# Differential heads' norm on the Scalar engine, rotations summed from PSUM, and a new order of the first block's tables, spreads and scores

## Chip, cores and metric

One core of a Trainium2 chip runs the whole program. The metric is the device time in microseconds of one execution, the median of several.

## What is computed

A three-layer stack on x of 512 tokens by 1024 channels, in fp32. Cut to what the change bears on:

```python
# first block
h = rms_norm(x, norm_mix); proj = h @ w_in            # pool, lru, q, k, v, gates
qh = rms_norm(q.reshape(B, S, 8, 128), q_norm)        # kh alike
z = qh @ kh.T * scale                                 # per head, causal
log_beta, log_keep = log_sigmoid(z), where(causal, log_sigmoid(-z), 0)
w = where(causal, exp(log_beta + reverse_cumsum_after(log_keep)), 0); y = w @ v
# ... pooling and LRU branches, gates, w_out, gated ffn
# even layer: MoBA attention (8 heads of 64) and differential attention (4 heads)
p = softmax(s)                                        # two score maps per head
o = rmsnorm((p[:, :, 0] - lam * p[:, :, 1]) @ v, subln_g) * (1 - lam_init)
# odd layer: dilated attention (8 heads of 64) and MLA (4 heads)
q = rmsnorm(cq, q_norm) @ w_uq                        # nope 128, rope 64 per head
rope(x) = [x1 * cos - x2 * sin, x1 * sin + x2 * cos]  # on q's rope part and on kr
# a convolutional ffn after each of both layers, then a last rmsnorm
```

## The kernel before

Channels lie on the 128 partitions (P) and the 512 tokens (S) in the free dimension; x is 8 tiles of 128x512 (KT = 8), and tokens are also counted in 4 blocks of 128 (NB). Each engine has its own program, written out by hand, and the programs meet at semaphores that count events. So the order of work on each engine is the order of the code, and an instruction that waits holds all behind it.

A product of full accuracy is three fp32r products of a high and a low part (L408 to L410, in the helper `products`). The high parts of the weights are made by ACT (L1306, in `refill`; L1428 while attention runs), the low parts by POOL (L1138), one slice of 128x2048 at a time, from raw weights that SP's DMA queue brings into two buffers.

**First block.** PE's loop over chunks of the value projection (i = 0, 1, with 4 blocks b of tokens, c for halves) weaves in the sums of squares of q and k (`qk_sum`, L852), and for i = 1 the 16 `qk_spread` products (L897), 2 per step: the reciprocal roots of 16 rows lie as high and low parts in rows 0 to 15 and 32 to 47 of `qkrstd`, the other rows being zero, and a product with a column of `both` spreads one of them over 128 partitions. DVE's `qk_norm` (L2221) then scales a tile of q or k, which gives `qk_normed`. ACT scales the values out of the banks (L1626, `v_read`), calling `refill` after each four. Then `sb_scores` (L938) of heads 0 and 1, products for the gates, `softplus` on ACT (L1642 to L1648), `sb_sums` (L950, L954), `sb_weights` (L1654). `token_scales` (L443) makes, in three places of the program, a column per block of tokens out of the row `rstd`; DVE copies it (L1862).

**Even layer.** Units g = 0 to 7 are the two score maps of each of the four differential heads, 8 to 15 are MoBA (`MOBA` = 8). For every head and block b of queries PE runs `transposes` of the merged weights, the scores of the next head's two units, `head_fill` (products of MoBA's queries, L408 to L410), and the products with the values (L655). ACT makes exponents (L1396) and copies even blocks of transposed weights from PSUM (L1418); DVE makes maxima (L1947), copies odd blocks (L1965, `copy_odd`), merges the two maps (L1974, L1975 and an addition) and, with `head_normalised`, scales the output by the sums. The norm of a head is `head_squares` (L1990, L1991, DVE), `diff_scales` (Ln and Exp, ACT) and `diff_normed` (L2007, DVE); `head_turn` then turns the head's tokens back (L726) on PE, ahead of both units of b = 2 one head later.

**Odd layer.** Units 16 to 23 are dilated attention (`DIL` = 16), 24 to 27 MLA. `SLOTS` is a table of what PE weaves in between the 32 steps (g, b) of the dilated units: `uq` products of MLA's queries in two halves (4 and 5 are the rope parts), `rot` the rotation product (0 for the keys, 1 and 2 for the queries, L762), `oturn` a turn of finished output, `uk` and `uv` keys and values. Results go to banks 7 and 2 in turn, in the order of `SPARE`, which all engines look up. ACT copies a finished `uq` out (`mla_copy`, L1516); DVE finishes a rotation in `rotated` (L2100, L2103, L2104: rotated part times sines, plain part times cosines, sum), at the step of its slot and ahead of the next `copy_odd`. `stack_low`, `key_low` and swaps of halves run on POOL (L1192, L1201).

## Time and profile before

| | us |
|---|---|
| median of 3 runs | 2227.19 (2226.87 to 2228.06) |
| the profiled execution | 2227.95 |
| its span | 2226.1 |
| busy PE, DVE, ACT, POOL | 2190.9, 875.4, 828.7, 1037.4 |

Rows of a timeline are: start, duration, engine, line, operation, out<-in, shapes, count, and in brackets the idle time of the engine before it with what ended it. MATMUL rows have modelled ends. PEld is the weight loads of PE. The span's average granted clock is 0.997 of full.

### The profile page before, as it was taken

What the parts mean: (1) busy time and instruction counts of PE and PEld (TensorE: products, weight loads), DVE (VectorE), ACT (ScalarE), POOL (GpSimd) and SP (SyncE); (2) the same over time, 40 slices, a digit from 0 to 9 for tenths busy, and PEclk for the clock granted to TensorE, in tenths of its full rate; (3) what the DMA queues carried; (4) which work ended last, traced back from release to release, by engine and by line L of the source; (5) the groups of instructions that cost most, each with busy time, mean ns of one, the idle gap of its engine ahead of it and who ended that gap; (6) DMA issues with size and microseconds to landing.
All of it is one profiled execution on the core that took longest, in us unless ns stands there. A gap on an engine that the chain in (4) does not pass through costs nothing. (4 is left out here: it accounts for less than half of the span.)

```text
span 2226.1 us, 27528 instructions
## 1 busy us (share of the span) xinstructions
PE 2190.9 (98%) x10090; PEld 1796.6 (81%) x10090; DVE 875.4 (39%) x1346; ACT 828.7 (37%) x1135; POOL 1037.4 (47%) x872
## 2 busy tenths in 40 slices
PE   8999999999999999999999999999999999999998
PEld 6768877888888888888878888888887788888887
DVE  6334576633351111222377533232225646332212
ACT  4235565422242222222246433332224634333321
POOL 5441144555554444555444354445554524444543
PEclk9999999999999999999999999999999999999999
DMA  5221122332223222333212222222332212222232
GB/s 172 92 77 57 42 91 77 113 107 99 97 76 113 94 94 77 104 103 108 96 54 66 76 95 94 101 89 91 100 120 90 72 48 95 94 95 94 84 104 77
DMA packets 33991, 201.88 MB, mean 91 GB/s; under 512 B 3900, under 2 KB 6204, under 8 KB 15484
## 3 DMA queue, kind: packets, MB, share of 16 engines
q1 hardware_dynamic: 31532, 192.94, 25.5%
q0 software_dynamic: 2384, 7.92, 1.2%
q8 instruction: 50, 0.82, 0.2%
q14 instruction: 25, 0.20, 0.0%
HBM read 198.69 MB, written 2.15 MB: 90 GB/s over the span
## 5 line engine op out<-in xcount | busy, mean ns | idle before, releaser
L1138 POOL TENSOR_TENSOR w_low<-raw,w_high 128x512 fp32r<-128x512 f32 (+2 forms) x768 | 959.8, 1281 | 1056.5 <-ACT w_high L1306 1013.4
L408 PE MATMUL bank<-x_low,w_high 128*128 128x512 f32 x1728 | 684.8, 396 | 10.7 <-DVE x_low L2141 9.3
L409 PE MATMUL bank<-x_high,w_high 128*128 128x512 f32 x1728 | 673.9, 390 | 0.0
L410 PE MATMUL bank<-x_high,w_low 128*128 128x512 f32 x1728 | 673.9, 390 | 0.0
L1306 ACT ACTIVATE w_high<-raw 128x2048 fp32r<-128x2048 f32 (+1 forms) x183 | 327.3, 1788 | 544.2 <-PE bank L410 544.2
L408 PEld LDWEIGHTS bank<-x_low,w_high 128*128 128x128 f32 x1728 | 325.3, 188 | 83.2 <-POOL w_low L1232 9.2
L409 PEld LDWEIGHTS bank<-x_high,w_high 128*128 128x128 f32 x1728 | 325.3, 188 | 70.4 <-issue 3.1
L410 PEld LDWEIGHTS bank<-x_high,w_low 128*128 128x128 f32 x1728 | 325.2, 188 | 68.6
L408 PE MATMUL bank<-act_low,w_high 128*128 128x512 f32 (+1 forms) x550 | 209.4, 381 | 0.0
L409 PE MATMUL bank<-act_high,w_high 128*128 128x512 f32 (+1 forms) x550 | 209.3, 381 | 0.0
L410 PE MATMUL bank<-act_high,w_low 128*128 128x512 f32 (+1 forms) x550 | 209.3, 380 | 0.0
L1928 DVE TENSOR_TENSOR temp_b<-temp_a,bank 128x512 f32<-128x512 f32 x66 | 45.4, 687 | 230.3 <-PE bank L410 229.9
L1371 ACT ACTIVATE act_high<-temp_b 128x512 f32 x66 | 41.8, 633 | 216.2 <-DVE temp_b L1928 216.0
L409 PEld LDWEIGHTS bank<-act_high,w_high 128*128 128x128 f32 x550 | 103.4, 188 | 19.8
L408 PEld LDWEIGHTS bank<-act_low,w_high 128*128 128x128 f32 x550 | 103.4, 188 | 19.8
L410 PEld LDWEIGHTS bank<-act_high,w_low 128*128 128x128 f32 x550 | 103.4, 188 | 19.7
L1882 DVE TENSOR_TENSOR gate_scaled<-bank,rstd 128x512 f32<-128x512 f32 x23 | 15.9, 692 | 257.2 <-PE bank L410 257.2
L1360 ACT ACTIVATE temp_a<-gate_scaled,columns 128x512 f32<-128x512 f32 x44 | 35.7, 816 | 157.9 <-DVE gate_scaled L1912 157.9
L1396 ACT ACTIVATE probs<-probs,small 128x128 f32<-128x128 f32 (+1 forms) x96 | 53.9, 561 | 100.6 <-DVE small L1947 100.2
L1912 DVE TENSOR_TENSOR gate_scaled<-bank,rstd 128x512 f32<-128x512 f32 x44 | 30.2, 691 | 152.7 <-PE bank L410 152.3
L408 PE MATMUL bank<-y_low,w_high 128*128 128x512 f32 x208 | 82.5, 397 | 0.0
L409 PE MATMUL bank<-y_high,w_high 128*128 128x512 f32 x208 | 80.9, 389 | 0.0
(284 smaller groups left out, 2745.9 us busy)
## 6 DMA issues: line engine op xcount, KB each, us to landing
raw<-wmain SPq DMA_DIRECT2D x144, 1024.0 KB, 4.9
raw<-wdown SPq DMA_DIRECT2D x48, 704.0 KB, 4.0
bias<-distance_table POOLq DMA_DIRECT2D x24, 256.0 KB, 3.4
raw<-wmain SPq DMA_DIRECT2D x4, 512.0 KB, 8.7
x_residual<-x SPq DMA_DIRECT2D x4, 512.0 KB, 7.4
out<-qk SPq DMA_DIRECT2D x8, 256.0 KB, 2.2
matrices<-mats SPq DMA_DIRECT2D x1, 512.0 KB, 11.5
r_blocks<-rg POOLq DMA_DIRECT2D x1, 512.0 KB, 6.4
```

The costliest lines, as they stand in the source:

```text
L408: pe.matmul(target, sh, ml, start=start and k == 0, stop=False)
L409: pe.matmul(target, sh, mh, start=False, stop=False)
L410: last = pe.matmul(target, sl, mh, start=False, stop=stop and k == n - 1)
L1138: pool.tensor_tensor(wl[:, c, part], raw[:, c, part], wh[:, c, part].bitcast(F32), ALU.subtract).then_inc(low_ready, 1)
L1306: act.activation(wh[:, c, 0:width], raw[:, c, 0:width], ACT.Copy).then_inc(high_ready, 1)
L1360: act.activation(tmpa[:, j, :], gs[:, j, :], ACT.Identity, bias=col("ffn_b", i * 2 + (k + j)), scale=col("ffn_w", i * 2 + (3 * k + 2 * FT ...
L1371: act.activation(tile(ah, i * 2 + j), tmpb[:, j, :], ACT.Copy).then_inc(sem("f_high"), 1)
L1396: act.activation(probs(g, b), probs(g, b), ACT.Exp, bias=nm[:, u, b:b + 1], scale=-1.0, accum_out=rs[:, u, b:b + 1]).then_inc(sem("p_ready ...
L1882: dve.tensor_tensor(gs[:, t % 2, :], bank[banks[t]][:, :], rstd[:, :], ALU.mult)\
L1912: dve.tensor_tensor(gs[:, j, :] if n else tmpa[:, j, :], bank[j][:, :], rstd[:, :], ALU.mult)\
L1928: dve.tensor_tensor(tmpb[:, j, :], tmpa[:, j, :], bank[2 + j][:, :], ALU.mult)\
```

## The change

- `token_scales`: four transposes of a 128x128 block of `rstd` instead of four fp32 products with one column; DVE's copy takes every 128th column.
- The spreads' operands have all 128 rows instead of 48; three spreads per step from the first step of i = 1 on instead of two per step.
- `sb_scores(0)` waits for 7 evictions of values instead of 8. ACT's table for Ln and Exp is loaded behind the Sqrt of `qk_std`; the second `refill` is moved behind `softplus(0)`.
- A differential head's norm: per block of tokens a Square with an accumulated sum, then Ln and Exp (b = 0 of the next head), then per block a Copy with a scale (b = 1), all on ACT; both DVE steps are gone. PE's `head_turn` is between the two units of b = 2. The ratio in `merge` is a tensor_scalar.
- Rotations: `key_parts` and `query_parts` on DVE multiply by cosines and by sines first, the queries straight from PSUM; PE rotates the sine part; `rotated` is one addition from PSUM. The order in `SLOTS` and `SPARE` follows.

```diff
@@ -81,7 +81,7 @@
              + [("eturn", 2), ("eturn", 3)] + [("eout", t) for t in range(6)]
-             + [("uq", 4), ("uq", 5), ("rot", 0), ("uq", 0), ("oturn", 0), ("rot", 1), ("uq", 1), ("rot", 2), ("uq", 2)]
+             + [("rot", 0), ("uq", 4), ("uq", 5), ("rot", 1), ("oturn", 0), ("uq", 0), ("rot", 2), ("uq", 1), ("uq", 2)]
              + [("oturn", 1), ("uq", 3)] + [("uk", j) for j in range(4)] + [("uv", 0), ("uv", 1), ("oturn", 2)]
@@ -89,10 +89,10 @@
 NONE = (None, 0, ())
-SLOTS = [("uq", 4, (0, 1)), ("uq", 5, (0,)), ("uq", 5, (1,)), NONE]
-SLOTS += [("rot", 0, ()), ("uq", 0, (0,)), ("uq", 0, (1,)), NONE]
-SLOTS += [("oturn", 0, ()), ("rot", 1, ()), ("uq", 1, (0,)), ("uq", 1, (1,))]
-SLOTS += [("rot", 2, ()), ("uq", 2, (0,)), ("uq", 2, (1,)), NONE]
+SLOTS = [("rot", 0, ()), ("uq", 4, (0,)), ("uq", 4, (1,)), NONE]
+SLOTS += [("uq", 5, (0,)), ("uq", 5, (1,)), ("rot", 1, ()), NONE]
+SLOTS += [("oturn", 0, ()), ("uq", 0, (0,)), ("uq", 0, (1,)), ("rot", 2, ())]
+SLOTS += [("uq", j, (k,)) for j in (1, 2) for k in range(2)]
 SLOTS += [("oturn", 1, ()), ("uq", 3, (0,)), ("uq", 3, (1,)), ("uk", 0, ())]
@@ -171,8 +171,8 @@
     ident_r, negtri_r, negones_r, negmask_r = (exact[:, j, :] for j in range(4))
-    qkrstd = over("qk_rstd_parts", [48, S], 40, F32R)
-    both = over("both_parts", [48, 16], 42.25, F32R)
+    qkrstd = over("qk_rstd_parts", [P, S], 40, F32R)
+    both = over("both_parts", [P, 16], 42.25, F32R)
@@ -194,7 +194,7 @@
-    turned = place("turned_rope", [P, S], at=mla_qk_at + KT * S * 4)
+    sines = place("sine_parts", [P, 2, S], at=mla_qk_at + KT * S * 4)
     qs_r = over("q_stage_r", [P, 2, S], 38, F32R)
@@ -440,8 +440,8 @@
                 for b in range(NB):
-                    last = pe.matmul(bank[target][:, b:b + 1], rstd[:, b * P:(b + 1) * P], ident[:, 0:1],
-                                     start=True, stop=True)
+                    tokens = slice(b * P, (b + 1) * P)
+                    last = pe.transpose(bank[target][:, tokens], rstd[:, tokens], ident)
                 last.then_inc(sem("token_scales"), 1)
@@ -618,7 +618,7 @@
                         spare_free(pe, ("uv", 2), ("uv", 3))
-                        pe.wait_ge(sem("roped"), 3)
+                        pe.wait_ge(sem("roped"), 9)
                     pe.matmul(target, mla_qk[:, 2 * m + u, q], mla_qk[:, 4 + 2 * m + u, 0:n], start=True, stop=False)
@@ -664,7 +664,7 @@
                 target = spare(("eturn", h))
-                pe.wait_ge(sem("y_token"), h + 1)
+                pe.wait_ge(sem("y_token"), 4 * h + 4)
                 turn(target, 4 + h).then_inc(sem("spare_ready"), 1)
@@ -680,9 +680,9 @@
                         transposes(2 * h, b)
-                        if 0 < h < HEADS - 1 and b == 2:
-                            head_turn(h - 1)
                         for u in range(2):
+                            if 0 < h < HEADS - 1 and b == 2 and u == 1:
+                                head_turn(h - 1)
                             if h < HEADS - 1:
@@ -757,9 +757,8 @@
-                if n:
-                    spare_free(pe, ("uq", 3 + n))
-                pe.matmul(spare(("rot", n)), small_rot, qk[:, 11 + n, :], start=True, stop=True)\
+                pe.wait_ge(sem("roped"), (2, 5, 7)[n])
+                pe.matmul(spare(("rot", n)), small_rot, sines[:, n - 1, :] if n else pts[:, 1, :], start=True, stop=True)\
                   .then_inc(sem("spare_ready"), 1)
@@ -894,7 +893,7 @@
                     pe.wait_ge(sem("qk_rstd"), 1)
-                pe.matmul(bank[4 + n % 4][:, :], both[:, t:t + 1].to_broadcast([48, P]), qkrstd[:, :], start=True,
+                pe.matmul(bank[4 + n % 4][:, :], both[:, t:t + 1].to_broadcast([P, P]), qkrstd[:, :], start=True,
                           stop=True).then_inc(sem("qk_spread"), 1)
@@ -917,8 +916,9 @@
                         if i == 1:
-                            qk_spread(8 * c + 2 * b)
-                            qk_spread(8 * c + 2 * b + 1)
+                            at = 4 * c + b
+                            for n in range(min(3 * at, 16), min(3 * at + 3, 16)):
+                                qk_spread(n)
@@ -931,7 +931,7 @@
                 else:
-                    pe.wait_ge(sem("v_read"), 8)
+                    pe.wait_ge(sem("v_read"), 7 + h)
                     pe.wait_ge(sem("qk_normed"), 16)
@@ -1163,7 +1163,7 @@
                         spare_free(pool, ("uq", 2), ("uq", 3))
-                        pool.wait_ge(sem("roped"), 3)
+                        pool.wait_ge(sem("roped"), 9)
                     pool.tensor_copy(gs[half, u, :], qk[half, n + 12, :]).then_inc(sem("rope_staged"), 1)
@@ -1456,8 +1456,10 @@
                             exponent(MOBA, b)
-                        if h and b == h // 3:
+                        if h and b == 0:
                             diff_scales(h - 1)
+                        if h and b == 1:
+                            diff_normed(h - 1)
                         if 0 < h < HEADS - 1 and b == 2:
@@ -1476,18 +1478,31 @@
                         spare_out(g, b)
-                        if (g, b) == (MOBA, 1):
+                        if (g, b) == (MOBA, 0):
                             diff_scales(3)
+                        if (g, b) == (MOBA, 2):
+                            diff_normed(3)
                         if b % 2:
...
                 d = dss[:, 4 * h:4 * h + 4]
-                act.wait_ge(sem("diff_squares"), h + 1)
+                act.wait_ge(sem("y_read"), h + 1)
+                for q in range(NB):
+                    act.activation(tmpa[:, 1, q * P:(q + 1) * P], yt[:, q, (4 + h) * P:(5 + h) * P], ACT.Square,
+                                   accum_out=d[:, q:q + 1]).then_inc(sem("diff_squares"), 1)
+                act.wait_ge(sem("diff_squares"), 4 * h + 4)
                 act.activation(d, d, ACT.Ln, bias=col("eps", 0), scale=1.0 / P).then_inc(sem("diff_scale"), 1)
...
                 act.activation(d, d, ACT.Exp, scale=-0.5).then_inc(sem("diff_scale"), 1)
+
+            def diff_normed(h):
+
+                act.wait_ge(sem("diff_scale"), 2 * h + 2)
+                for q in range(NB):
+                    y = yt[:, q, (4 + h) * P:(5 + h) * P]
+                    act.activation(y, y, ACT.Copy, scale=dss[:, 4 * h + q:4 * h + q + 1]).then_inc(sem("y_token"), 1)
@@ -1529,8 +1544,8 @@
                     kind, n, ks = SLOTS[at]
-                    if kind == "uq" and 1 in ks:
-                        mla_copy(("uq", n), qk[:, 8 + n, :] if n >= 4 else mla_qk[:, n, :], scale=192 ** -0.5)
+                    if kind == "uq" and n < 4 and 1 in ks:
+                        mla_copy(("uq", n), mla_qk[:, n, :], scale=192 ** -0.5)
                     elif kind == "oturn":
@@ -1620,12 +1635,14 @@
                     act.activation(gs[0:16, 0, :], gs[0:16, 0, :], ACT.Sqrt).then_inc(sem("qk_std"), 1)
+                    act.preload_act_table_set("natural_log_exp_and_others")
                 for b in range(NB):
...
                        .then_inc(sem("v_read"), 1)
-                refill(1, n0 + 2 * i + 1)
+                if i == 0:
+                    refill(1, n0 + 1)
             act.wait_ge(table_stored, 16)
@@ -1658,8 +1675,9 @@
-            act.preload_act_table_set("natural_log_exp_and_others")
             softplus(0)
+            act.wait_ge(sem("v_ready"), 10)
+            refill(1, n0 + 3)
             softplus(1)
@@ -1859,7 +1877,7 @@
                 dve.wait_ge(sem("token_scales"), n)
-                dve.tensor_copy(token_rstd, bank[source][:, 0:NB]).then_inc(sem("token_copied"), 1)
+                dve.tensor_copy(token_rstd, bank[source][:, 0:S:P]).then_inc(sem("token_copied"), 1)
                 dve.wait_ge(sem("token_copied"), n)
@@ -1972,7 +1990,7 @@
                 step(dve.reciprocal(rd2, rs[:, :, b:b + 1]))
-                step(dve.scalar_tensor_tensor(ratio, rs[:, 0, b:b + 1], nlam, rd2[:, 1, :], ALU.mult, ALU.mult))
+                step(dve.tensor_scalar(ratio, rs[:, 0, b:b + 1], nlam, rd2[:, 1, :], ALU.mult, ALU.mult))
                 dve.scalar_tensor_tensor(probs(2 * h, b), probs(2 * h + 1, b), ratio, probs(2 * h, b), ALU.mult,
@@ -1982,13 +2000,6 @@
                                   ALU.mult).then_inc(sem("y_read"), 1)
-
-            def head_squares(h):
-
-                y, w = yt[:, :, (4 + h) * P:(5 + h) * P], blocks(tmpa[:, 1, :])
-                dve.wait_ge(sem("y_read"), h + 1)
-                step(dve.tensor_tensor(w, y, y, ALU.mult))
-                dve.tensor_reduce(dss[:, 4 * h:4 * h + 4].unsqueeze(2), w, AX.X, ALU.add).then_inc(sem("diff_squares"), 1)
@@ -1999,13 +2010,6 @@
                    .then_inc(sem("y_read"), 1)
-
-            def diff_normed(h):
-
-                dve.wait_ge(sem("diff_scale"), 2 * h + 2)
-                y = yt[:, :, (4 + h) * P:(5 + h) * P]
-                dve.tensor_tensor(y, y, dss[:, 4 * h:4 * h + 4].unsqueeze(2).to_broadcast([P, NB, P]), ALU.mult)\
-                   .then_inc(sem("y_token"), 1)
@@ -2039,17 +2043,11 @@
                             moba_copy(0)
-                        if h == HEADS - 1 and b == 0:
-                            head_squares(h - 1)
-                        if h and b == 1 + h // 3:
-                            diff_normed(h - 1)
                         if 0 < h < HEADS - 1 and b == 3:
...
                     head_normalised(h)
-                    if h < 2:
-                        head_squares(h)
@@ -2064,10 +2062,6 @@
                             stack_low(g + 2, b - 1)
-                        if (g, b) == (MOBA, 0):
-                            head_squares(3)
-                        if (g, b) == (MOBA, 2):
-                            diff_normed(3)
                         spare_out(g, b)
@@ -2091,18 +2085,31 @@
+            def key_parts():
+
+                x = qk[:, 11, :]
+                dve.wait_ge(sem("rope_landed"), 16)
+                dve.tensor_tensor(pts[:, 1, :], x, rope[:, 1, :], ALU.mult).then_inc(sem("roped"), 1)
+                dve.tensor_tensor(x, x, rope[:, 0, :], ALU.mult).then_inc(sem("roped"), 1)
+
+            def query_parts(n):
+
+                use = ("uq", 3 + n)
+                dve.wait_ge(sem("spare_ready"), SPARE[use] + 1)
+                dve.scalar_tensor_tensor(qk[:, 11 + n, :], spare_bank(use), 192 ** -0.5, rope[:, 0, :], ALU.mult, ALU.mult)\
+                   .then_inc(sem("roped"), 1)
+                dve.scalar_tensor_tensor(sines[:, n - 1, :], spare_bank(use), 192 ** -0.5, rope[:, 1, :], ALU.mult,
+                                         ALU.mult).then_inc(sem("roped"), 1)
+                dve.wait_ge(sem("roped"), 2 * n + 3)
+                dve.sem_inc(spare_read(use), 1)
+
             def rotated(n):
-                x, use = qk[:, 11 + n, :], SPARE["rot", n]
-                if n == 0:
-                    dve.wait_ge(sem("rope_landed"), 16)
-                dve.wait_ge(sem("spare_ready"), use + 1)
-                dve.tensor_tensor(turned[:, :], spare_bank(("rot", n)), rope[:, 1, :], ALU.mult)\
-                   .then_inc(spare_read(("rot", n)), 1)
-                spare_free(dve, ("rot", n))
-                step(dve.tensor_tensor(x, x, rope[:, 0, :], ALU.mult))
-                dve.tensor_tensor(x, x, turned[:, :], ALU.add).then_inc(sem("roped"), 1)
-                dve.wait_ge(sem("roped"), n + 1)
+                x, use = qk[:, 11 + n, :], ("rot", n)
+                dve.wait_ge(sem("spare_ready"), SPARE[use] + 1)
+                dve.tensor_tensor(x, x, spare_bank(use), ALU.add).then_inc(spare_read(use), 1)
+                spare_free(dve, use)
+                dve.sem_inc(sem("roped"), 1)
@@ -2115,11 +2122,13 @@
                     at = 4 * (g - DIL) + b
-                    kind, n, _ = SLOTS[at]
+                    kind, n, ks = SLOTS[at]
                     if at and SLOTS[at - 1][0] == "oturn":
...
                         rotated(n)
+                    elif kind == "uq" and n >= 4 and 1 in ks:
+                        query_parts(n - 3)
                 elif (g, b) == (MLA, 1):
@@ -2204,7 +2213,7 @@
             dve.sem_inc(table_ready, 1)
-            step(dve.tensor_tensor(both[:, :], ident[0:48, 0:16], ident[0:48, 32:48], ALU.add))
+            step(dve.tensor_tensor(both[:, :], ident[:, 0:16], ident[:, 32:48], ALU.add))
             step(dve.memset(qkrstd[:, :].bitcast(F32), 0.0))
@@ -2391,6 +2400,7 @@
                 stack_low(g, 1)
+            key_parts()
             dve.wait_ge(sem("c_sum"), 3)
...
                 dve.tensor_scalar(tq[:, 2 + t, :], bank[6 + t][:, :], 1.0 / (2 * P, P)[t], EPS, ALU.mult, ALU.add)\
```

## Rows read from the trace of the kernel before

**Rows 1.** Part 1 of the page: busy time, share of the span, instructions.
```profile
PE 2190.9 (98%) x10090; PEld 1796.6 (81%) x10090; DVE 875.4 (39%) x1346; ACT 828.7 (37%) x1135; POOL 1037.4 (47%) x872
```
**Rows 2.** Timeline of PE and its weight loads, a pair of spreads (start, us, ...).
```profile
155.80 0.39 PE L409 MATMUL bank<-w_high,x_high 128*128 128x512 f32 x1
156.02 0.39 PE L410 MATMUL bank<-w_high,x_low 128*128 128x512 f32 x1
156.34 0.29 PEld L897 LDWEIGHTS bank<-qk_rstd_parts,both_parts 48*128 48x128 f32 x2 [0.35 <-issue]
...
157.34 0.40 PE L409 MATMUL bank<-w_high,x_high 128*128 128x512 f32 x1
```
**Rows 3.** Timeline of PE: scores of heads 0 and 1, and a later head's.
```profile
159.63 0.39 PE L410 MATMUL bank<-w_high,x_low 128*128 128x512 f32 x1
...
162.03 6.24 PE L938 MATMUL bank<-qk 128*128 128x512 f32 x16 [1.35 <-DVE qk L2221]
167.93 0.58 PE L408 MATMUL bank<-x_low,w_high 128*128 128x512 f32 x1
...
208.37 2.32 PE L938 MATMUL bank<-qk 128*128 128x512 f32 x8
210.52 2.32 PE L964 MATMUL bank<-sb_weights,v_tokens 128*128 128x512 f32 x8
```
**Rows 4.** Timeline of ACT between the values and the first softplus.
```profile
160.64 1.90 ACT L1306 ACTIVATE w_high<-raw 128x2048 fp32r<-128x2048 f32 x1
162.56 1.28 ACT L1661 ACT_TABLE_LOAD   x1
```
**Rows 5.** Windows: busy us of PE, PEld, DVE, ACT, POOL; PEclk, DMA share, GB/s.
```profile
162.20:165.70 3.50, 3.50 (x7) 1.86 (x7) 0.00 (x0) 2.30 (x4) 3.08 (x3) 0.51 0.00 0
1169.10:1172.60 3.50, 3.48 (x12) 3.18 (x13) 2.56 (x7) 1.97 (x7) 0.00 (x0) 0.51 0.62 255
1140.00:1160.00 20.00, 17.86 (x89) 14.06 (x88) 16.02 (x35) 9.51 (x25) 11.32 (x10) 1.00 0.19 66
```
**Rows 6.** Timeline of PE: the first token_scales.
```profile
75.96 0.95 PE L443 MATMUL bank<-matrices,rstd 128*128 128x1 f32 x8
76.78 0.40 PE L852 MATMUL bank<-square_high,pick_r 128*16 128x512 f32 x1
```
**Rows 7.** Timeline of PE, differential heads: the rows in front of which it waits.
```profile
1129.10 0.63 PE L726 MATMUL bank<-matrices,y_tokens 128*128 128x128 f32 x4 [0.57 <-DVE y_tokens L2007]
...
1150.59 0.63 PE L726 MATMUL bank<-matrices,y_tokens 128*128 128x128 f32 x4 [2.14 <-DVE y_tokens L2007]
...
1169.12 1.20 PE L655 MATMUL bank<-v_tokens,probs_t 128*128 128x128 f32 x4 [3.13 <-DVE probs_t L1965]
...
1187.81 1.77 PE L655 MATMUL bank<-v_tokens,probs_t 128*128 128x64 f32 x14 [0.83 <-ACT probs_t L1418]
```
**Rows 8.** Timeline of DVE in the differential heads.
```profile
1160.25 0.22 DVE L1975 SCALAR_TENSOR_TENSOR small<-small 128x1 f32<-128x1 f32 x1
...
1163.36 1.21 DVE L1975 SCALAR_TENSOR_TENSOR small<-small 128x1 f32<-128x1 f32 x1
...
1166.27 1.74 DVE L1990 TENSOR_TENSOR temp_a<-y_tokens 128x512 f32<-128x512 f32 x1
```
**Rows 9.** Timeline of ACT in the differential heads: an exponent of 128x128.
```profile
1143.32 0.40 ACT L1396 ACTIVATE probs<-probs,small 128x128 f32<-128x128 f32 x1 [2.17 <-DVE small L1947]
```
**Rows 10.** PE's waits in 1712 to 1751: us in total, times, longest.
```profile
PE bank L655 <- DVE probs_t L1965: 1.8, 2, 1.2
PE bank L655 <- ACT probs_t L1418: 1.7, 3, 0.6
PE bank L408 <- DVE qk_r L2085: 0.7, 1, 0.7
```
**Rows 11.** Timeline of DVE, dilated stage: rotated's third operation.
```profile
1726.81 1.66 DVE L2104 TENSOR_TENSOR qk<-qk,turned_rope 128x512 f32<-128x512 f32 x1
```
**Rows 12.** ACT by lines, 1238 to 1268: count, busy us and mean ns, idle before.
```profile
L1323 ACT ACTIVATE temp_a<-x_residual 128x512 f32<-128x512 f32 x8 | 4.9, 616 | 0.0
```

## Prediction, written before the changed kernel was run

> **What bounds the kernel now.** I read the page's busy shares first: PE is busy for 98% of the span, each other engine for less than half of it [rows 1]. So only what PE does or waits for can move the end, and I went on to PE's waits, then to the timeline of the three places that the diff touches. One caution for all of it: a 512-column product starts 0.22 to 0.23 us after the one before (155.80, 156.02), though its row shows 0.39, with a modelled end [rows 2]. An idle in a row is counted from that late end, so a stall costs about 0.17 more than the row says. I sum starts, not idles.
>
> **Part 1, first block.** *Spreads.* Two `qk_spread` products run between products in each block of tokens. From 156.02 to 157.34 is 1.32 us, in which the pair and two products start; four at 0.227 would be 0.91. The other 0.41 goes with the 0.35 that stands, as "issue", in front of the weights' load of 48 rows [rows 2]; loads of 128 rows around it have none. With 128 rows the load has its neighbours' form, so I drop 0.41 for the 7 pairs ahead of the last: **2.9 us** (bounds 0, and 3.3 for all 8). The Trainium skill, "TensorE: Matmul & The Clock Gate", section "Step-by-step: what each phase is for", speaks against it: load time goes by columns, and the number of rows doesn't matter. By that rule this term is 0 and the time 2.9 higher; the 0.35 in front of the 48-row load is what I go by.
>
> *The gap.* With three spreads per block, the last pair leaves the place where it delays everything. From 159.63 to 162.03 is 2.40 us where 0.23 is the pace; 0.45 of it is the pair, which runs earlier now: 2.40 - 0.23 - 0.45 = **1.7 us** [rows 3]. The wait inside it, 1.35 for DVE's `qk` L2221, goes because the last row is normalised a block earlier, and `sb_scores(0)` no longer stands for the eviction of the last v bank (7 for 8). What is late next is `softplus(0)`: ahead of it on ACT stood a refill of 1.90 and a table load of 1.28 [rows 4]. The load moves to the values' stage, where ACT idles between evictions, and the refill behind `softplus(0)`, so the chain ends about when PE comes to `sb_sums(0)`: 0, and at most 1.9 back if that cover fails. The slice refilled is wanted two heads later: no wait.
>
> *Scores.* The 16 records of heads 0 and 1 take 162.03 to 167.93, 5.90 us; the 8 of a later head 208.37 to 210.52, 2.15, so 16 should take 4.30 [rows 3]. Why: the granted clock is 0.51 of full, 1.2 of 2.4 GHz, for 3.5 us right behind the wait [rows 5]. Without the wait I expect no fall: 1.6 and 0.2 in the product behind, **1.8 us** (bounds 0 and 1.8).
>
> *Tables.* `token_scales` at 75.96 takes 0.82 up to the next start, for 8 one-column records [rows 6]. Four 128-column transposes lie at 0.63 with their modelled tail of some 0.2 (the `head_turn` rows in [rows 7]), so about 0.45: **0.4 us**. At the two later places the copy stands behind DVE's evictions anyway: 0. Part 1: 2.9 + 1.7 + 1.8 + 0.4 = **6.8**.
>
> **Part 2, differential heads.** PE stands here for DVE at 1129.10 (0.57) and 1150.59 (2.14), both for `diff_normed` L2007, and at 1169.12 (3.13), for `probs_t` L1965, which is late because DVE's queue is [rows 7]. With the hidden 0.17 that is 0.74, 2.3 and 3.3. DVE is full: 16.0 of 20 us [rows 5]. The squares L1990 take 1.74, and the ratio L1975 takes 0.22 once and 1.21 three us on, with POOL making low halves beside it [rows 8]. Squares, their sum and `diff_normed` leave DVE, some 3 to 4 us a head. I keep 0.4 of the 2.3 and 0.3 of the 3.3, since the turn now waits for four copies on ACT: 0.74 + 1.9 + 3.0 = 5.6. With the wait at 1169 its half clock goes too, 3.5 us at 0.51 [rows 5]: **1.7**.
>
> ACT gets four squares with their sums and four copies of 128x128 per head. An exponent of that size with the reading of its sum is 0.40 [rows 9]; a copy has no sum to read, an estimate of 0.27: 4 x 0.40 + 4 x 0.27 = 2.7 us a head. ACT was busy for 9.5 of 20 us [rows 5], so this is covered on the average. Where PE already stands for ACT, 0.83 at 1187.81 [rows 7], a little grows: -0.3. On PE `head_turn` moves between the two units of b = 2; behind its new wait (`y_token` 4h + 4) stand the scores of u = 1 and `head_fill`. Part 2: 5.6 + 1.7 - 0.3 = **7.0**, bounds 3 and 9.
>
> *The ratio* as one tensor and two per-partition scalars: between 0 and the 1.0 of [rows 8] a time, already within the 3.0. The Trainium skill, "SBUF — State Buffer", section "Who interferes with whom", says that two SBUF inputs contend with POOL's reads, as 1.21 against 0.22 bears out; but also that tensor_scalar can take the shared port as a whole and then block. By the latter the edit gives nothing, and the time would be some 0.5 higher.
>
> **Part 3, dilated stage (1712 to 1751).** PE's waits are 5.7 us by the rows in ten waits, of which three lines stand in [rows 10]; ten times 0.16 more makes 7.3. (a) The 0.7 for `qk_r` L2085 is that of slot 0, the `uq4` product; now the keys' rotation is first, ready long before: 0.8. (b) The `mla_copy` of `uq4` and `uq5` leave ACT, where they stand ahead of `probs_t` L1418: of three waits (1.7) I drop 1.1. (c) `rotated` is three operations on DVE, of which the last, with both inputs in SBUF, takes 1.66 [rows 11], and a `copy_odd` (L1965) is behind them; one sum from PSUM remains. Both its waits go: 1.8 + 0.3 = 2.1. (d) The wait for L1947: 0.3. Together **4.3**, bounds 2 and 6. What comes instead: `query_parts`, two PSUM operations of some 0.7 each in front of a `copy_odd`; and `key_parts`, ahead of the wait for `c_sum`, which pushes the low halves and the values' evictions by 1.4 us or more, an estimate at the two rates of an SBUF pair. PE wants these later than that. `roped` 9 instead of 3 in the MLA scores is met some units before: 0.
>
> **Sum.** 6.8 + 7.0 + 4.3 = 18.1 off the profiled execution's own 2227.95 gives 2209.85. That execution is 0.76 above the runs' median of 2227.19, so **2209.1**.
>
> **Rivals.** (1) *ACT becomes the bound in the heads.* Squares stand at b = 0 and copies at b = 1, ahead of that block's next exponents and copies, so PE stands for ACT where it stood for DVE; an average of half says nothing of one block. Part 2 is then 0 instead of 7: 2216.1 (2213 to 2219). For it: the 0.83 at 1187.81; against it: 9.5 of 20 us. (2) *DVE or POOL bounds the dilated stage.* The 1.4 us of `query_parts` takes the place of what goes, or POOL's bias and key halves are what is late next, and Part 3 gives 1: 2212.4. (3) *The number of rows is irrelevant*, and the 0.41 comes from the broadcast weights or from the place, which stay: 2209.1 + 2.9 = 2212.0. The skill's rule above would say so. (4) *The clock falls elsewhere*, behind new waits, as often as now: 2209.1 + 3.4 = 2212.5. (5) **Slower:** *the tables of ACT are loaded anew in every head.* If Square or Copy lay in another set than Exp and Ln, each head had two loads at 1.28 [rows 4] with the 2.7 of work between exponents that PE waits for, 5.3 us; times 4 is 21, and Part 2's gain is gone as well: 2209.1 + 7 + 21 = 2237. It decides where ACT's idle in a head is under 5.3 in one piece. Against it: eight Squares of L1323 run between others of ACT with 0.0 idle before them [rows 12], and a load is a row of its own, which that stretch lacks. (6) *The change doesn't do what it says*: new waits hold the moved steps where the old ones did, and Parts 2 and 3 are nil: 2227.2 - 6.8 = 2220.4.
>
> **How the numbers follow.** Main case 0.55 (2205 to 2213.5); (1) 0.17, (2) 0.11, (3) 0.05, (4) 0.04, (5) 0.03, (6) or several together 0.05. A difference under 0.2%, 4.5 us, is about what can't be told from none here. So faster is all under 2222.7: main and (1) to (4), 0.92. Same 0.05: (6) alone would still be a little under that line, but Part 1's lower bounds (0 for the spreads, 0 for the scores) carry it over, and I count it whole. Slower 0.03, from (5). The range takes (1) to (4) in: up to 2218, and down to 2203, where the upper bounds of the three parts (7.2 + 9 + 6 = 22.2, so 2205.0) stand, with 2 us for waits that I haven't counted.
>
> **What would show it.** Right: no "issue" ahead of the spreads' loads; less than 0.5 between the last product and L938 of head 0; a clock of 1.0 in both stretches; no wait of PE for y_tokens over 0.5; the one addition left of `rotated` near 0.7; PE's waits in the dilated stage at 2 or less. Wrong: PE standing for L1418 or L1396 over 2 us in all between 1100 and 1190 (rival 1); table loads in the heads (rival 5); a wait for softplus in front of `sb_sums(0)` of over 0.5; a wait at L628 or L655 of the dilated stage that falls on `query_parts`. What makes all of it wrong is a stretch that the change lengthens where I saw no wait.

## The result and the profile after

The changed kernel takes 2216.84 us (2213.99 to 2217.16, 5 runs) where the kernel before took 2227.19; the ratio is 0.9950, 95% interval 0.9939 to 0.9962. So 10.3 us came off, where 18.1 were forecast. The profiled execution is 2217.16 us with a span of 2215.3, the slowest of the five; beside the profiled 2227.95 of before it is 10.8 less. The page's first part, as [rows 1] before:

```profile
PE 2185.9 (99%) x10078; PEld 1797.6 (81%) x10078; DVE 861.8 (39%) x1334; ACT 838.7 (38%) x1181; POOL 1038.8 (47%) x872
```

DVE lost 13.6 us of work and ACT gained 10.0. What PE stands for is told by its waits over the whole span (us in total, times, longest); the first three lines and those of the places touched:

```profile
PE bank L408 <- DVE x_low L2150: 9.5, 1, 9.5
PE bank L950 <- DVE softplus_low L2270: 2.9, 1, 2.9
PE bank L408 <- PEq L431: 1.9, 2, 1.1
PE bank L655 <- ACT probs_t L1418: 1.6, 3, 0.8
...
PE bank L655 <- DVE probs_t L1983: 1.5, 2, 1.3
...
PE bank L726 <- DVE y_tokens L2010: 0.8, 2, 0.5
```

The waits for `diff_normed` are gone. The second line is new: `sb_sums(0)` stands 2.9 us for DVE.

To see where the time went I took the start of the same product of PE in each trace: the 1401st of its L409 rows, shortly ahead of the differential heads, and the 1501st, shortly behind them. The three stretches that they cut tell the three parts of the change apart:

| us | up to the 1401st | from there to the 1501st | from there to PE's last row |
|---|---|---|---|
| before | 1065.06 | 109.95 | 1044.59 |
| after | 1063.97 | 102.80 | 1041.87 |
| difference | -1.1 | -7.2 | -2.7 |
| forecast | -6.8 | -7.0 | -4.3 |

The heads are right to 0.2 us, the first block is nearly all missing, and the dilated stage lacks 1.6.

One thing has to come off the first column. The first work of PE that the change touches is the first `token_scales`, and PE comes to it at 75.96 before and at 75.29 after, so 0.7 of the 1.1 is a difference of the two executions and not of the change. From there to the 1401st product it is 989.10 us before and 988.69 after: 0.4 less.

**First block, after.** The timeline of PE shows the changed `token_scales`, and three spreads between two products; PE's gap ahead of the scores of head 0 is gone. It answers to [rows 6], [rows 2] and [rows 3]:

```profile
75.29 0.60 PE L444 MATMUL bank<-matrices,rstd 128*128 128x128 f32 x4
75.64 0.48 PE L851 MATMUL bank<-square_high,pick_r 128*16 128x512 f32 x1
...
133.56 0.86 PE L896 MATMUL bank<-qk_rstd_parts,both_parts 128*128 128x512 f32 x3
134.25 0.39 PE L408 MATMUL bank<-w_low,x_high 128*128 128x512 f32 x1
...
156.14 0.39 PE L410 MATMUL bank<-w_high,x_low 128*128 128x512 f32 x1
156.37 4.48 PE L938 MATMUL bank<-qk 128*128 128x512 f32 x16
160.50 0.58 PE L408 MATMUL bank<-x_low,w_high 128*128 128x512 f32 x1
...
169.19 0.50 PE L950 MATMUL bank<-softplus_high,matrices_r 128*128 128x512 f32 x1 [2.85 <-DVE softplus_low L2270]
```

Start to start, `token_scales` takes 0.35 (before 0.82), three spreads 0.69, which is three times the pace, the step from the last product to the scores 0.23, the scores 4.13 (before 5.90). All as forecast. Together, from the first `token_scales` to the scores, PE takes 81.08 us where it took 86.07: 5.0 less, as forecast. Then comes the wait. The scores have the full clock, and the window right behind the wait has half of it (columns as in [rows 5]), for 6.8 us, where the kernel before had 3.4 at its scores:

```profile
156.30:160.50 4.20, 4.20 (x19) 2.59 (x17) 0.00 (x0) 3.49 (x8) 0.00 (x0) 1.00 0.00 0
...
170.80:174.20 3.40, 3.40 (x16) 3.40 (x16) 3.30 (x8) 1.20 (x3) 0.53 (x1) 0.50 0.82 248
174.20:177.60 3.40, 3.40 (x9) 2.63 (x9) 0.38 (x2) 0.38 (x1) 0.00 (x0) 0.51 0.94 374
```

Why DVE is late is in its own timeline and POOL's. First the kernel before, DVE then POOL:

```profile
170.88 0.90 DVE L2258 CAST softplus_high<-softplus 128x1024 fp32r<-128x1024 f32 x2
171.81 1.56 DVE L2261 TENSOR_TENSOR softplus_low<-softplus,softplus_high 128x1024 fp32r<-128x1024 f32 x2
...
162.62 4.94 POOL L1138 TENSOR_TENSOR w_low<-raw,w_high 128x512 fp32r<-128x512 f32 x4 [9.97 <-ACT w_high L1306]
```

and the same of the changed kernel:

```profile
163.50 2.00 DVE L2267 CAST softplus_high<-softplus 128x1024 fp32r<-128x1024 f32 x2
165.54 3.60 DVE L2270 TENSOR_TENSOR softplus_low<-softplus,softplus_high 128x1024 fp32r<-128x1024 f32 x2
...
163.73 6.55 POOL L1138 TENSOR_TENSOR w_low<-raw,w_high 128x512 fp32r<-128x512 f32 x4 [12.68 <-ACT w_high L1306]
```

Before, POOL's slice ended (167.6) ahead of DVE's casts (170.9). Now the moved refill releases it at 163.7, and it lies exactly beside them: 2.46 us of DVE work takes 5.60, 3.1 more, and POOL's 4.94 takes 6.55. That 3.1 covers the wait of 2.85; the experiments below test it.

**Heads, after.** The windows (columns as in [rows 5]) and PE's waits, both of 1095 to 1190:

```profile
1095.00:1190.00 95.00, 93.49 (x521) 76.34 (x520) 62.68 (x179) 61.95 (x187) 43.28 (x44) 1.00 0.20 65
```
```profile
PE bank L655 <- ACT probs_t L1418: 0.8, 1, 0.8
PE bank L408 <- DVE qk L2072: 0.4, 1, 0.4
PE bank L628 <- issue: 0.2, 1, 0.2
```

In the kernel before the same window had the waits of [rows 7] and this balance:

```profile
1095.00:1190.00 95.00, 87.99 (x470) 71.35 (x469) 73.34 (x180) 47.72 (x125) 39.14 (x39) 0.98 0.19 62
```

ACT went from 47.7 to 62.0 busy us, and PE stands for it 0.8 us, as before. Some of that is that the same window now holds more of the program (521 records of PE instead of 470). The reader should note that DVE's and ACT's shares are now nearly equal, 66% and 65%.

**Dilated stage, after.** PE's waits in 1700 to 1745, against the 5.7 of which [rows 10] has three lines:

```profile
PE bank L655 <- DVE probs_t L1983: 1.3, 1, 1.3
PE bank L726 <- DVE y_tokens L2010: 0.5, 1, 0.5
PE bank L655 <- ACT probs_t L1418: 0.4, 1, 0.4
PE bank L628 <- DVE small L1965: 0.3, 1, 0.3
PE bank L628 <- issue: 0.3, 1, 0.3
```

2.8 us are left. Behind the longest, which ends at 1721.57, is again half a clock:

```profile
1723.80:1727.20 3.40, 3.40 (x16) 3.11 (x14) 2.35 (x7) 2.71 (x7) 2.45 (x4) 0.50 0.28 43
```

### The profile page after: what moved, and what is told of

Read it like the earlier page. It is cut to its first block, busy times and chain, and to the rows that moved or that the text cites. A ratio compares the mean times of both kernels' runs of the same rounds, so it can differ in the third digit from the quotient of the medians.

```text
span 2215.3 us, 27545 instructions
## 1 busy us (share of the span) xinstructions
PE 2185.9 (99%) x10078; PEld 1797.6 (81%) x10078; DVE 861.8 (39%) x1334; ACT 838.7 (38%) x1181; POOL 1038.8 (47%) x872
## 4 chain that ended last, share of the span: by engine, by line
PE 95%; DVE 2%; ACT 1%; issue 0%; DMA 0%; POOL 0%; DVEq 0%; SPq 0%; PEldq 0%; ACTq 0%
PE bank L408 29%; PE bank L409 28%; PE bank L410 28%; PE bank L655 2%; PE bank L950 1%; PE bank L642 1%; PE bank L625 1%; PE bank L964 1%; DVE pool_a L2346 1%; PE bank L938 1%; PE bank L622 0%; PE bank L623 0%; PE bank L628 0%; PE bank L629 0%; PE bank L851 0%
## 5 line engine op out<-in xcount | busy, mean ns | idle before, releaser
L408 PE MATMUL bank<-x_low,w_high 128*128 128x512 f32 x1728 | 684.6, 396 | 11.4 <-DVE x_low L2150 9.5
L409 PE MATMUL bank<-x_high,w_high 128*128 128x512 f32 x1728 | 674.0, 390 | 0.0
L408 PEld LDWEIGHTS bank<-x_low,w_high 128*128 128x128 f32 x1728 | 325.4, 188 | 84.7 <-POOL w_low L1232 9.5
L409 PEld LDWEIGHTS bank<-x_high,w_high 128*128 128x128 f32 x1728 | 325.5, 188 | 70.1 <-issue 3.1
L408 PE MATMUL bank<-act_low,w_high 128*128 128x512 f32 (+1 forms) x550 | 209.4, 381 | 0.0
L409 PE MATMUL bank<-act_high,w_high 128*128 128x512 f32 (+1 forms) x550 | 209.3, 381 | 0.0
L1946 DVE TENSOR_TENSOR temp_b<-temp_a,bank 128x512 f32<-128x512 f32 x66 | 45.4, 688 | 229.1 <-PE bank L410 228.8
L408 PEld LDWEIGHTS bank<-act_low,w_high 128*128 128x128 f32 x550 | 103.4, 188 | 19.9
L409 PEld LDWEIGHTS bank<-act_high,w_high 128*128 128x128 f32 x550 | 103.4, 188 | 19.6
L408 PE MATMUL bank<-y_low,w_high 128*128 128x512 f32 x208 | 82.5, 397 | 0.0
L1396 ACT ACTIVATE probs<-probs,small 128x128 f32<-128x128 f32 (+1 forms) x96 | 53.8, 561 | 74.1 <-DVE small L1965 73.5
L409 PE MATMUL bank<-y_high,w_high 128*128 128x512 f32 x208 | 80.9, 389 | 0.0
```

Of the source, the lines that this page charges most:

```text
L408: pe.matmul(target, sh, ml, start=start and k == 0, stop=False)
L409: pe.matmul(target, sh, mh, start=False, stop=False)
L1396: act.activation(probs(g, b), probs(g, b), ACT.Exp, bias=nm[:, u, b:b + 1], scale=-1.0, accum_out=rs[:, u, b:b + 1]).then_inc(sem("p_ready ...
L1946: dve.tensor_tensor(tmpb[:, j, :], tmpa[:, j, :], bank[2 + j][:, :], ALU.mult)\
```

## Experiments

Two theories stood at the start. **A**: each part does what was forecast, but the moved refill puts POOL's low halves beside DVE's softplus halves, and the wait and the halved clock behind it cost the first block its gain. **B**: the first block's win is whole and the parts take it from each other later; or DVE's chain is too long for a PE that comes 6 us sooner, whatever POOL does.

**One part at a time.** The kernel before, with one part of the diff each.

First block alone, e1_block1 (the hunks on `token_scales`, spreads, `sb_scores`, `preload_act_table_set` and `refill`):

> The kernel before with the first block's part alone. Theory A (what the trace after shows): the part wins about 6.7 us up to the last score of head 1 and loses 3.0 in a wait of PE for softplus_low and up to 3.4 to a halved clock right behind it, so about 1.1 in all: 2226 us, and a wait at L950 of about 2.9. Rival B: the first block's win is whole (6.8) and what is missing in the changed kernel is lost later, through an interplay of the parts: 2220.4 and no wait at L950.

Measured: 2226.05 us (2224.62 to 2231.17, 11 runs) beside 2227.17 of before, ratio 0.9998 (0.9989 to 1.0007). The wait is there, `PE bank L951 <- DVE softplus_low L2265: 2.9, 1, 2.9` in its list; the half clock behind it lasts 3.4 us in this execution, where it lasted 6.8 in the changed kernel's. So the loss is the part's own and needs no interplay; B's first half falls.

Heads alone, e2_heads (the hunks on `diff_scales`, `diff_normed`, `head_squares`, `head_turn` and `merge`):

> The kernel before with the differential heads' part alone (norm on the Scalar engine, the ratio as tensor_scalar, the turn between the units). Theory A: 7.2 us off as the stretch 1094 to 1230 is shorter by in the trace after, so 2220.0; no halved clock near 1165. Rival B, the Scalar engine becomes the bound: 0 to 2 us off, waits for probs_t L1418 or the exponents of over 2 us in all.

Measured: 2219.71 us (2217.92 to 2221.19, 6 runs), ratio 0.9968 (0.9955 to 0.9980). 7.5 us off by the medians (7.1 by the ratio); the stretch of the heads is 102.82 us in it, as in the changed kernel (102.80). PE's waits for L1418 are 3.0 in all over its whole span (before 2.9). ACT is not the bound.

Rotations and slots alone, e3_rotations (`SLOTS`, `SPARE`, `key_parts`, `query_parts`, `rotated`, `rotate`, `roped`):

> The kernel before with the rotations' part and the order of slots alone. Theory A: 4.3 us off less a halving of the clock behind the wait for probs_t L1965 in unit 17 (1.7), so 2.5 off: 2224.7. Rival B: the halving doesn't come when the stretches ahead are as in the kernel before, 4.3 off: 2222.9. Rival C: DVE's query_parts take back what goes, 1 off or less: 2226 or more.

Measured: 2222.79 us (2221.86 to 2223.07, 11 runs), ratio 0.9982 (0.9973 to 0.9991). 4.4 us off: rival B of this run, no halving in the stretch. From the 1501st product to PE's last row it is 1040.64 us, 4.0 less than before. So the forecast of 4.3 was nearly right for the work. Of the 1.6 missing in the changed kernel's profile, 1.2 (1041.87 against 1040.64) go with its halved clock and 0.3 to 0.4 are work that didn't go.

**The refill behind softplus(1), e4_refill_late.** One edit on the changed kernel:

```diff
             softplus(0)
-            act.wait_ge(sem("v_ready"), 10)
-            refill(1, n0 + 3)
             softplus(1)
+            act.wait_ge(sem("v_ready"), 10)
+            refill(1, n0 + 3)
```

> The changed kernel with the first block's second refill behind softplus(1) instead of between softplus(0) and softplus(1). Theory A: the 2.9 us wait of PE at L950 is that of DVE's low halves of the softplus (3.60 us for two, with POOL's w_low beside it); with POOL's slice later these two take about 1.6, the wait goes under 0.5 and the halved clock behind it goes too: 2216.8 - 3.0 - 3.4 = 2210.4. Rival B: DVE's chain is too long for a PE that comes 6 us earlier, whatever POOL does: the wait stays over 2 and the time within 0.5 of 2216.8. Rival C: the wait goes but a new one comes at the sums of head 1, where POOL's slice now stands beside DVE: 2213 to 2215.

Measured: 2210.79 us (2209.51 to 2211.54, 5 runs), ratio to before 0.9927 (0.9913 to 0.9940). Theory A to 0.4 us. From the first `token_scales` to the 1401st product it is 982.38 us, 6.3 less than the 988.69 of the changed kernel. The timeline of DVE and of POOL in it:

```profile
163.82 0.90 DVE L2267 CAST softplus_high<-softplus 128x1024 fp32r<-128x1024 f32 x2
164.75 1.56 DVE L2270 TENSOR_TENSOR softplus_low<-softplus,softplus_high 128x1024 fp32r<-128x1024 f32 x2
...
168.95 2.05 DVE L2263 TENSOR_TENSOR softplus<-softplus,matrices 128x384 f32<-128x384 f32 x2
171.04 2.96 DVE L2267 CAST softplus_high<-softplus 128x1024 fp32r<-128x1024 f32 x2
...
167.99 5.86 POOL L1138 TENSOR_TENSOR w_low<-raw,w_high 128x512 fp32r<-128x512 f32 x4 [16.61 <-ACT w_high L1306]
```

The same pair of operations has its old 0.90 and 1.56, and PE starts `sb_sums(0)` at 166.50 with no wait. The stretching moved with POOL's slice to head 1: the mask operations L2263 take 2.05 (0.76 for head 0), the casts 2.96. It costs nothing there: the halves are made at 175.6, PE comes for those sums at 179.43, and its list has no wait at L950. Rival C falls. This version beats both kernels; its slowest run (2211.54) is under the fastest of the changed kernel (2213.99).

**The refill where it was, e8_refill_early.** The changed kernel, with `refill` behind the last value again, ahead of `softplus(0)`:

```diff
-                if i == 0:
-                    refill(1, n0 + 1)
+                refill(1, n0 + 2 * i + 1)
...
-            act.wait_ge(sem("v_ready"), 10)
-            refill(1, n0 + 3)
             softplus(1)
```

> The changed kernel with the second refill where it was in the kernel before, behind the last value and ahead of softplus(0). Theory A: POOL's slice is then made ahead of DVE's low halves of the softplus, which take 1.6 for two again, but the whole chain is 1.9 later by the refill on ACT: the wait at L950 is 2.9 - 3.1 + 1.9, about 1.7, and the time 2213 to 2216. Rival B: only ACT's order counted, and the wait is 2.9 + 1.9 = 4.8: 2218 or more.

Measured: 2212.57 us (2212.04 to 2213.08, 5 runs), ratio 0.9936 (0.9923 to 0.9950). Its DVE and PE timelines:

```profile
166.66 1.56 DVE L2267 TENSOR_TENSOR softplus_low<-softplus,softplus_high 128x1024 fp32r<-128x1024 f32 x2
...
168.28 0.50 PE L950 MATMUL bank<-softplus_high,matrices_r 128*128 128x512 f32 x1 [1.03 <-DVE softplus_low L2267]
```

The halves take 1.56 again, and the wait is 1.03: the refill's 1.9 on ACT, less what slack there was. I had expected 1.7 and 2213 to 2216, too much; no half clock follows this shorter wait. Rival B, a wait of 4.8, falls: ACT's order alone doesn't explain the loss. So moving the refill as the change does was the one step that cost: its old place is 4.3 us better (2216.84 against 2212.57), a later one 6.0 (2210.79).

**The row count of the spreads, e5_late_rows48.** As the version with the late refill, but `qk_rstd_parts` and `both_parts` with 48 rows again, three spreads per step as changed:

```diff
-    qkrstd = over("qk_rstd_parts", [P, S], 40, F32R)
-    both = over("both_parts", [P, 16], 42.25, F32R)
+    qkrstd = over("qk_rstd_parts", [48, S], 40, F32R)
+    both = over("both_parts", [48, 16], 42.25, F32R)
...
```

> As e4_refill_late, but with the spreads' operands of 48 rows again, still three per step. Theory A: what costs is the 48-row load; 0.35 of issue comes back in front of each of the six groups and the time is 2 to 3 us above that of e4_refill_late (2210.8), so 2213.3. Rival B: the number of rows is irrelevant and the changed order took the issue away: within 0.3 of 2210.8, no issue in front of L896.

Measured: 2212.53 us (2211.99 to 2213.56, 5 runs) against 2210.79. The loads and products of one step in its timeline:

```profile
133.97 0.53 PEld L896 LDWEIGHTS bank<-qk_rstd_parts,both_parts 48*128 48x128 f32 x3 [0.35 <-issue]
...
133.65 0.39 PE L410 MATMUL bank<-w_high,x_low 128*128 128x512 f32 x1
133.97 0.97 PE L896 MATMUL bank<-qk_rstd_parts,both_parts 48*128 48x512 f32 x3
134.86 0.50 PE L408 MATMUL bank<-w_low,x_high 128*128 128x512 f32 x1
```

The 0.35 is back with nothing but the rows changed. The 1401st product starts 2.5 us later than with 128 rows (1060.53 against 1057.99), and PE reached the first `token_scales` at 75.61 in both; that is 0.42 for each of the six groups. The medians differ by 1.7, the ratios' intervals overlap, and the runs' ranges don't. The late refill's profiled execution has a halved clock in the dilated stage and this one has none, so its profiled time gives back some of the 2.5. It is theory A (2 to 3) by the traces and a little under it by the medians; rival B falls. The Trainium skill's rule that the number of rows doesn't matter for the time of a load ("TensorE: Matmul & The Clock Gate", section "Step-by-step: what each phase is for") agrees with the rows of the loads themselves, 0.18 for one of 48 rows and 0.19 for one of 128. What the 48 rows cost stands between the loads, and the reading of the rule by which this term would be 0 doesn't hold here.

**The ratio, e7_late_stt.** As the version with the late refill, but

```diff
-                step(dve.tensor_scalar(ratio, rs[:, 0, b:b + 1], nlam, rd2[:, 1, :], ALU.mult, ALU.mult))
+                step(dve.scalar_tensor_tensor(ratio, rs[:, 0, b:b + 1], nlam, rd2[:, 1, :], ALU.mult, ALU.mult))
```

> As e4_refill_late, with the ratio of the two score maps as a scalar_tensor_tensor again. Theory A: its mean goes from 0.27 back to over 0.5 us, at most 1 us at a time on DVE; DVE has room now that squares and norm are gone, so the time rises by 0 to 0.5 over 2210.8. Rival B: this edit carried most of the heads' gain: 2212.5 or more, and a wait for probs_t L1983 of 1 us or more near 1160.

Measured: 2211.55 us (2210.83 to 2213.20, 5 runs), 0.8 over the late refill's 2210.79; within the spread of the two. DVE by lines in 1085 to 1185, this version and then the one with tensor_scalar:

```profile
L1993 DVE SCALAR_TENSOR_TENSOR small<-small 128x1 f32<-128x1 f32 x16 | 8.6, 537 | 0.6
```
```profile
L1993 DVE TENSOR_SCALAR small<-small 128x1 f32<-128x1 f32 x16 | 4.4, 274 | 0.6
```

The mean halves. In the heads the trace has a wait of 0.8 for `probs_t` L1983 that the other lacks, and 1.0 instead of 0.5 at L408; the stretch between the 1401st and the 1501st product is 104.61, where the six traces with the heads' part and tensor_scalar lie between 102.78 and 102.82. So the edit carries about 1.8 of the heads' 7.2, more than theory A's 0.5 in the trace, far from rival B's main share. Row by row, scalar_tensor_tensor takes 0.22 with POOL idle and 0.37 to 1.20 beside it. The one-column tensor_scalar operations keep their 0.27 in all 16 rows, of which nine lie beside POOL's work; the Trainium skill's remark that tensor_scalar may take the shared port and block ("SBUF — State Buffer", section "Who interferes with whom") is not seen in these rows.

**The rotation a slot later, e6_late_rot7.** As the version with the late refill, with

```diff
-SLOTS += [("uq", 5, (0,)), ("uq", 5, (1,)), ("rot", 1, ()), NONE]
+SLOTS += [("uq", 5, (0,)), ("uq", 5, (1,)), NONE, ("rot", 1, ())]
```

> As e4_refill_late, with the rotation of the first query pair in slot 7 instead of 6. Theory A: the wait of 1.3 at L655 (unit 17, block 3) is for a copy_odd that stands behind rotated(1) on DVE, 0.69 and 0.23 us; with rotated(1) behind that copy it is 0.9 shorter and the halved clock behind it goes in part of the executions: 2208.5 to 2209.9. Rival B: the copy is held by the maxima of unit 18 (0.56 behind a wait of its own for PE), so the wait stays over 1.0 and the time within 0.4 of 2210.8.

Measured: 2210.35 us (2210.18 to 2210.82, 5 runs), 0.4 under the late refill's: no difference that can be told, and outside theory A's 2208.5 to 2209.9. In its timeline, PE and then POOL:

```profile
1714.94 1.10 PE L655 MATMUL bank<-v_tokens,probs_t 128*128 128x64 f32 x8 [0.36 <-DVE probs_t L1983]
...
1717.36 0.30 PE L628 MATMUL bank<-temp_b_r,q_stage_r 128*128 128x128 f32 x1 [1.20 <-issue]
...
1714.66 1.26 POOL L1192 TENSOR_TENSOR temp_b_r<-qk,temp_b_r 64x512 fp32r<-64x512 f32 x1
1715.98 1.28 POOL L1201 CAST temp_a_r<-q_stage_r 64x512 fp32r<-64x512 f32 x2
```

The wait for the copy fell from 1.3 to 0.36, as theory A says, so rival B's reason is out too. But a wait of 1.20 came at the next scores. The profile names no releaser for it; they start 0.10 after POOL's casts end (1717.26), and in the changed kernel the same scores also start 0.10 after those casts (1723.06 and 1722.96). I read it as POOL standing behind DVE with nearly the same deadline. This is the mechanism of rival (2) of the prediction, at one place.

## Why the forecast came out as it did

- **Spreads, 2.9**: right. It was 0.41 for each of seven pairs; undoing the rows alone costs 0.42 for each of six groups, 2.5 by the traces (1.7 by the medians).
- **The gap, 1.7, and token_scales, 0.4**: right, and with the spreads 5.0 as measured (86.07 to 81.08); 0.23 from the last product to L938, and 0.47 for the first `token_scales`.
- **What is late next behind the gap**: here the mechanism of the prediction failed. It checked the moved refill on ACT ("the chain ends about when PE comes") and, for the slice, only when PE wants it. It left out who works while POOL makes that slice. The refill's low halves are released by it, 5 us of POOL work that used to end before DVE's casts and now lies beside them. Rows for the price were at hand: [rows 8] had 1.21 against 0.22 for the same effect. The bound given, "at most 1.9 back", was also wrong, since it named only ACT. The cost was 3.0 of waiting (2.85 by the row) plus the clock behind it, 6.3 together (988.69 against 982.38). The list of signs did name this place, a wait for softplus in front of `sb_sums(0)` of over 0.5, but no rival went with it, and no price beyond the 1.9.
- **The first halving of the clock, 1.8**: the scores ran at full clock, but with a new wait of 3 us the clock fell behind that one, for 6.8 us instead of 3.4. The term was also taken from one execution as if it were the rule: with the first block unchanged and the same wait of 1.35 at the scores, the profiled executions of heads alone and of rotations alone have no fall there, and take 1.4 us less from the first `token_scales` to the 1401st product (987.74 and 987.76 against 989.10). Rival (4) had falls elsewhere at 3.4 for all places, with a chance of 0.04: too low, since waits of over 1 us are left. Two new falls, about 3.4 in the first block and 1.2 in the dilated stage, stand against two old ones gone (1.4 and about 1.7).
- **With the refill moved out of DVE's way**, the time to the 1401st product is 7.1 less than before, and counted from the first `token_scales` 6.7 less (982.38 against 989.10), with 6.8 forecast.
- **Heads, 7.0**: right, 7.2 in the traces and 7.5 by the part alone. The four squares with their sums take 1.27 (0.29 from one start to the next; forecast 1.60) and the four copies 1.28 as one row (1.08), in sum about what was priced. The turn didn't wait for ACT's copies, for which the forecast kept 0.4 and 0.3; that 0.4 at L408 for DVE's `moba_copy` and 0.2 at L628 stand there instead is a size that came out by luck. The ACT-bound wait didn't grow. ACT's table wasn't loaded again: rival (5) fell as its rows said.
- **Dilated stage, 4.3**: nearly right for the part alone (4.4, or 4.0 in the trace). The sum named (c), both L1965 waits, as gone; one of 1.3 stayed, because `rotated(1)` with a pause (0.68 and 0.23) still stands ahead of `copy_odd`, and POOL is nearly as late. (d), the 0.3 for the maxima, also stayed, and a wait of 0.5 for `y_tokens` L2010 is new in the stage. `query_parts` brought no wait of its own.
- **In sum** 6.3 for the new wait with the clock behind it, 1.2 of clock in the dilated stage, and 0.4 of its work: 18.1 - 6.3 - 1.2 - 0.4 is 10.2, against 10.3. That the time lay in the range (2203 to 2218) is luck as far as the first block goes: 2216.84 is where rival (1) was put (2213 to 2219), and its sign, PE standing over 2 us for L1418 or L1396 in the heads, was 0.8. The range took in rivals of this size though not this one.
- **Signs**: met were no issue ahead of the spreads, 0.23 ahead of L938, a clock of 1.0 at the scores and in the heads, no wait for `y_tokens` over the 0.5 of the list, and 0.68 for `rotated`'s addition. Missed were the wait ahead of `sb_sums(0)` (2.85 against 0.5) and PE's waits in the dilated stage (2.8 against 2).

What stays open: why the clock falls behind some waits and not behind the same ones in another execution. Over the ten traces a fall follows the wait of 3.1 at L655 in three of three and that of 2.85 ahead of `sb_sums(0)` in two of two; the 2.1 at L726 in one of three, the 1.35 ahead of the scores in one of three, and the 1.2 to 1.3 at L655 in the dilated stage in four of nine. The changed kernel's own runs differ in the same way: 2213.99 and 2214.50 at a mean clock of 0.998, and 2216.84 to 2217.16 at 0.996. So the 6.3 is the loss of an execution with the long fall; with the fall of 3.4 us, as in the first block alone, it is about 4.7 (987.08 against 982.38).

## What to carry to other kernels

When a step is moved, list not only its own engine's queue but all work that it releases, and look who runs beside that work at its new time: here 1.9 us on ACT released 5 us on POOL, which slowed DVE by 3.1 on the path. When a wait is removed, the engine comes earlier everywhere behind it, so the whole chain that it will wait for next is to be laid beside its new arrival, with stretched durations as well as with clean ones. A gain that rests on a fall of the clock seen in one profile comes only in the executions that had the fall: here 1.4 us in one of three traces with the same wait.

## What the runs showed of the hardware

- DVE and POOL slowed each other where DVE's operands all lay in SBUF: the casts L2267 took 0.90 for two alone and 2.00 or 2.96 beside POOL, the subtractions L2270 1.56 and 3.60; POOL's slice 4.94, 5.86 and 6.55. DVE's operations with one source in PSUM didn't stretch. The softplus operation with a bank as one source (L2258 in the late refill, L2255 in the early one) takes 1.62 for three with POOL idle and 1.62 wholly beside POOL's slice. Over the whole trace of the changed kernel L1946, one source in a bank, has a mean of 0.69 in 35 rows wholly beside POOL's work and in 31 without it; L1916, both sources in SBUF, has 1.43 in 25 and 0.68 in 16.
- A load of weights with 48 rows has 0.35 us of issue ahead of it between loads of 128 rows, and costs 0.41 to 0.42 a group from product to product; with 128 rows and zeros it has neither.
- Executions of one kernel differ by whole falls of the clock: those of the first block alone lie from 2224.62 at a mean clock of 0.998 to 2231.17 at 0.994. A difference of 2 us between two kernels can be one fall, so it is to be read from a stretch of the trace without one.
